# One prologue stage for the input transposes, the bias vectors, the conditioning and the first two weight blocks

## The reference

```python
proj = jnp.einsum('bsd,df->bsf', h, w_in).astype(jnp.float32)
qa, ka, va, qb, kb, vb, lr_f, lr_b, gate = _split(proj, (A_WIDTH, A_WIDTH, A_WIDTH, B_K_WIDTH, ...))
oa = dilated_attention(heads(qa, A_HEADS), heads(ka, A_HEADS), heads(va, A_HEADS), rel_bias)
...
bias = jnp.transpose(rel_bias.astype(jnp.float32)[_t5_bucket(off * dilation)], (2, 0, 1))
s = jnp.einsum('brnqhe,brnkhe->brnhqk', qs, kb) * (E ** -0.5) + bias
```

## Time and profile before

| | |
|---|---|
| median of 3 runs | 4393.03 us (4392.2 to 4393.21) |
| profiled execution | 4389.74 us, span 4388.0 us |
| TensorE, matmul busy | 3691.0 us, 84% of the span |
| VectorE / ScalarE / GpSimd busy | 1654.2 / 1069.0 / 1010.2 us |
| `tin`: first issue to last copy | 0.83 to 24.33 us |
| `bv`: first issue to the issue of the next stage | 25.04 to 35.32 us |
| `cond`: the same | 35.32 to 39.48 us |
| `in0`: first issue, first matmul | 39.48 us, 44.84 us |
| mean granted TensorE clock | 0.909 |

### The profile page before, as it was taken

One profiled execution on the slowest core, in us unless ns is written; L12 is line 12 of the kernel. 1 busy time (PEld: TensorE's weight loads), 2 busy tenths in 40 slices (PEclk: granted clock), 3 DMA queues, 4 the chain that ended last, 5 costly groups with the idle time before them and its releaser, 6 DMA issues. The chain is left out here.

```text
span 4388.0 us, 47384 instructions
## 1 busy us (share of the span) xinstructions
PE 3691.0 (84%) x16689; PEld 2400.1 (55%) x16689; DVE 1654.2 (38%) x3948; ACT 1069.0 (24%) x2172; POOL 1010.2 (23%) x844
## 2 busy tenths in 40 slices
PE   7989997887889999999998798976877835667996
PEld 3645776666445666756667346463557735333442
DVE  1025552332441343354451450063479447131101
ACT  0023433331332233233331440022214101111111
POOL 0000001332331333343342451001312534111110
PEclk8999998999999999999999897997988858888998
DMA  3164532223421111111112522253325520445996
GB/s 107 58 177 137 166 99 87 89 68 110 170 106 55 48 51 47 46 48 35 47 56 90 203 108 81 75 156 94 110 79 164 180 85 25 168 182 182 319 324 222
DMA packets 423889, 510.55 MB, mean 116 GB/s; under 512 B 71778, under 2 KB 327290, under 8 KB 423667
## 3 DMA queue, kind: packets, MB, share of 16 engines
q1 hardware_dynamic: 390067, 467.26, 32.3%
q10 hardware_dynamic: 28992, 23.65, 1.6%
q0 software_dynamic: 4608, 16.78, 1.5%
HBM read 372.94 MB, written 134.66 MB: 116 GB/s over the span
## 5 line engine op out<-in xcount | busy, mean ns | idle before, releaser
L634 PE MATMUL hgrn_ps_w<-xT,hgrn_ring 128*128 128x512 f32 x1152 | 509.8, 598 | 0.0
L606 POOL TENSOR_TENSOR hgrn_queries<-hgrn_qd,hgrn_pair_decay 128x640 f32<-128x640 f32 x192 | 285.0, 1502 | 418.2 <-PE hgrn_ps_a L685 200.0
L634 PEld LDWEIGHTS hgrn_ps_w<-xT,hgrn_ring 128*128 128x128 f32 x1152 | 218.1, 193 | 252.9 <-issue 252.8
L630 PE MATMUL hgrn_ps_w<-hgrn_ring,xT 128*128 128x256 f32 x1536 | 337.8, 379 | 0.0
L630 PEld LDWEIGHTS hgrn_ps_w<-hgrn_ring,xT 128*128 128x128 f32 x1536 | 289.2, 190 | 38.0 <-issue 0.5
L786 DVE COPY_PREDICATED hgrn_scores<-hgrn_mask,hgrn_ps_s 128x128 f32<-128x128 uint32 x192 | 48.6, 297 | 474.1 <-issue 470.3
L358 PE MATMUL gla_bg_ps<-gla_bg_w,xT 128*128 128x256 f32 x768 | 195.9, 402 | 5.2 <-DMA gla_bg_w<-in_w_in_ab_dram 5.2
L358 PEld LDWEIGHTS gla_bg_ps<-gla_bg_w,xT 128*128 128x128 f32 x768 | 151.6, 202 | 38.5 <-issue 10.6
L1151 PE MATMUL end_ps_z<-end_w,end_yT 128*128 128x512 f32 x384 | 169.2, 601 | 1.6 <-ACT end_yT L1100 1.6
L2298 PE MATMUL end_ps_z<-end_w,end_yT 128*128 128x512 f32 x384 | 168.1, 598 | 0.8 <-ACT end_yT L2226 0.8
L884 ACT ACTIVATE hgrn_k_tok<-hgrn_ps_a 128x256 f32<-128x256 f32 x84 | 32.2, 383 | 549.8 <-PE hgrn_ps_a L660 549.8
(11 more groups left out here) (597 smaller groups left out, 6865.3 us busy)
## 6 DMA issues: line engine op xcount, KB each, us to landing
expw_wg<-in_exp_w_gate_dram SPq DMA_DIRECT2D x16, 2048.0 KB, 11.1
expw_wu<-in_exp_w_up_dram SPq DMA_DIRECT2D x16, 2048.0 KB, 16.3
expw_wd<-in_exp_w_down_dram SPq DMA_DIRECT2D x16, 2048.0 KB, 21.9
att_w_ada<-in_ada_w_dram SPq DMA_DIRECT2D x24, 1024.0 KB, 5.9
hgrn_ring<-in_w_in_c_dram SPq DMA_DIRECT2D x36, 512.0 KB, 4.1
end_gt<-gate_l SPq DMA_DIRECT2D x16, 768.0 KB, 7.3
hgrn_ring<-in_w_in_c_dram SPq DMA_DIRECT2D x12, 1024.0 KB, 5.5
hgrn_o<-hgrn_o_stage SPq DMA_DIRECT2D x192, 64.0 KB, 2.7
```

Source lines behind the costliest of these rows:

```text
L606: pool.tensor_tensor(queries[:, d, s, :].rearrange("p (b a c) -> p b a c", b=POINTS, a=PC), q, f, ALU.mult).then_inc(queries_done, 1)
L630: last = pe.matmul(bank[:, q * 2 * P:(q + 1) * 2 * P], xT[:, k, t * P:(t + 1) * P], wt[:, k, :], start=(k == 0), stop=(k == KB - 1))
L634: last = pe.matmul(bank[:, :], wt[:, k, 0:P], xT[:, k, part * BANK:(part + 1) * BANK], start=(k == 0), stop=(k == KB - 1))
```

## The change

The first three stages become one, `prologue`, which also loads the two first weight blocks of the projection. All 8 tiles of `x` have a buffer of their own and are issued at once, then the two weight blocks, `c` and `c_ctx`, and, once POOL has cleared the tile, the four blocks of zero rows, all from SP's queue. The bias table and the indicators are loaded from ScalarE's queue. TensorE uses 5 banks for the transposes and 3 for the bias matmuls, which stand behind tile 4. VectorE copies the even banks and ScalarE the odd ones. POOL sets the zeros and the row of ones. ScalarE does the SiLU behind its copies, then issues the store of `vectors` and waits for all five stores; SP waits for the weights. `project` gets the loaded buffers: it skips the loads of units 0 and 1 and shifts the counts of its waits for weights.

```diff
-def transpose_in(nc, tag, src, dst, rows):
+def prologue(nc, tag, src, dst, rel_bias, buckets, vectors, vpad, c, c_ctx, sT, weights, wbuf):
...
+        @block.sync
+        def _(sp):
+            for t in range(T):
+                sp.dma_start(raw[:, t, :], src[t * P:(t + 1) * P, :]).then_inc(raw_loaded[t], 16)
+            for b in range(2):
+                sp.dma_start(wbuf[b][:, :, :], weights.rearrange("(k p) n -> p k n", p=P)[:, :, b * W:(b + 1) * W]).then_inc(w_loaded, 16)
+            with nc.allow_non_contiguous_dma(reason="a vector goes down the partitions"):
+                sp.dma_start(cond[:, 0, :], c[0].rearrange("(k p) -> p k", p=P)).then_inc(cond_loaded, 16)
+                sp.dma_start(cond[:, 1, :], c_ctx.rearrange("(k p) -> p k", p=P)).then_inc(cond_loaded, 16)
+            sp.wait_ge(zeroed, 2)
+            for first in (0, P, VPAD + SEQ, VPAD + SEQ + P):
+                sp.dma_start(vpad[first:first + P, :], zero[:, :]).then_inc(stored, 16)
+            sp.wait_ge(w_loaded, 32)
...
+            pool.memset(zero[:, :], 0.0).then_inc(zeroed, 1)
+            pool.drain()
+            pool.memset(rb[REL_BUCKETS:REL_BUCKETS + 1, :], 1.0).then_inc(zeroed, 1)
+
+        @block.scalar
+        def _(act):
+            act.dma_start(rb[0:REL_BUCKETS, :], rel_bias).then_inc(bias_loaded, 16)
+            act.dma_start(bk[:, :], buckets).then_inc(bias_loaded, 16)
             for t in range(T):
...
+                n = 2 * t + 1
+                act.wait_ge(turned, n + 1)
+                act.activation(dst[:, 4:8, t * P:(t + 1) * P], ps[n % 5][:, :].rearrange("p (j c) -> p j c", j=4), ACT.Copy).then_inc(act_copied, 1)
+            act.wait_ge(cond_loaded, 32)
+            act.activation(sT[:, :, :], cond[:, :, :].rearrange("p r k -> p k r"), ACT.Silu)
+            act.wait_ge(scaled, 3)
+            act.dma_start(vectors, vec[:, :]).then_inc(stored, 16)
+            act.wait_ge(stored, 80)
...
+                if t == MIDDLE:
+                    pe.wait_ge(bias_loaded, 32)
+                    pe.wait_ge(zeroed, 2)
+                    for n in range(3):
+                        pe.matmul(ps_v[n][0:AH, 0:VEC], rb[:, :], bk[:, n * VEC:(n + 1) * VEC], start=True, stop=True).then_inc(made, 1)
...
-def project(nc, tag, jobs, columns=None):
+def project(nc, tag, jobs, columns=None, loaded=None):
...
-        wbuf = [sb(f"wbuf{b}", [P, KB, W]) for b in range(2)]
+        wbuf = loaded or [sb(f"wbuf{b}", [P, KB, W]) for b in range(2)]
+        held = 2 if loaded else 0
...
+                if u < held:
+                    return
...
-                wait(pe, w_loaded[u % 2], 16 * i + 16 * (u // 2 + 1))
+                wait(pe, w_loaded[u % 2], 16 * i + 16 * (u // 2 + 1) - 8 * held)
```

More of the change, by code:

```diff
@@ L49, in make_identity @@
     pool.drain()
-def transpose_in(nc, tag, src, dst, rows):
-    T = rows // P
+def prologue(nc, tag, src, dst, rel_bias, buckets, vectors, vpad, c, c_ctx, sT, weights, wbuf):
+    T = SEQ // P
+    W = wbuf[0].shape[2]
     with ExitStack() as ctx:
@@ L57, in transpose_in @@
         sem = own_semaphores(nc, ctx, tag)
[L58 removed]
+        raw = sb("raw", [P, T, D])
         ident = sb("ident", [P, P])
[L60 to L63 removed]
+        rb, bk = sb("rb", [REL_BUCKETS + 1, AH]), sb("bk", [REL_BUCKETS + 1, 3 * VEC])
+        zero = sb("zero", [P, AH * AE])
+        vec = sb("vec", [AH, 3 * VEC])
+        cond = sb("cond", [P, 2, KB])
+        ps = [ctx.enter_context(nc.psum_tensor(f"{tag}_ps{b}", [P, BANK], F32)) for b in range(5)]
+        ps_v = [ctx.enter_context(nc.psum_tensor(f"{tag}_ps_v{n}", [P, BANK], F32)) for n in range(3)]
+        raw_loaded = [sem(f"raw_loaded{t}") for t in range(T)]
+        ident_ready, turned, dve_copied, act_copied = sem("ident_ready"), sem("turned"), sem("dve_copied"), sem("act_copied")
+        bias_loaded, zeroed, made, scaled, stored = sem("bias_loaded"), sem("zeroed"), sem("made"), sem("scaled"), sem("stored")
+        cond_loaded, w_loaded = sem("cond_loaded"), sem("w_loaded")
+        block = ctx.enter_context(nc.Block())
+        MIDDLE = T // 2
+        @block.sync
[11 more added lines that the diff above has]
+            sp.wait_ge(w_loaded, 32)
         @block.gpsimd
@@ L92, in _ @@
             for t in range(T):
[L93 to L97, removed]
+                n = 2 * t
+                dve.wait_ge(turned, n + 1)
+                dve.tensor_copy(dst[:, 0:4, t * P:(t + 1) * P], ps[n % 5][:, :].rearrange("p (j c) -> p j c", j=4)).then_inc(dve_copied, 1)
+                if t == MIDDLE + 1:
+                    for n in range(3):
+                        dve.wait_ge(made, n + 1)
+                        dve.tensor_scalar(vec[:, n * VEC:(n + 1) * VEC], ps_v[n][0:AH, 0:VEC], 8.0, None, ALU.mult).then_inc(scaled, 1)
 CHANNEL, TOKEN = "channel", "token"
@@ L1284, in bucket_constant @@
     return out[:, :, ::-1]
[L1287 to L1325, removed]
 def dilated_attention(nc, tag, qT, kT, vpad, vectors, attn, jobs, sT, ada_w, ada):
@@ L2056, in _ @@
             bg.move(act, LEAD + 3 * STEPS)
-def condition(nc, tag, c, c_ctx, sT):
-    with ExitStack() as ctx:
-        raw = ctx.enter_context(nc.sbuf_tensor(f"{tag}_raw", [P, 2, KB], F32))
-        loaded = own_semaphores(nc, ctx, tag)("loaded")
-        block = ctx.enter_context(nc.Block())
-        @block.sync
-        def _(sp):
-            with nc.allow_non_contiguous_dma(reason="a vector goes down the partitions"):
-                sp.dma_start(raw[:, 0, :], c[0].rearrange("(k p) -> p k", p=P)).then_inc(loaded, 16)
-                sp.dma_start(raw[:, 1, :], c_ctx.rearrange("(k p) -> p k", p=P)).then_inc(loaded, 16)
-        @block.scalar
-        def _(act):
-            act.wait_ge(loaded, 32)
-            act.activation(sT[:, :, :], raw[:, :, :].rearrange("p r k -> p k r"), ACT.Silu)
 def close_and_modulate(nc, tag, x, x_next, hT, context, hcT, o, gate, gain, w_out, ln_gain, ln_bias, alpha, norm_g, ada, ada_bias):
@@ L4421, in network @@
         gla_o = [dram(f"gla_o{d}", SEQ, B) for d in range(2)]
-        bias_vectors(nc, "bv", rel_bias, buckets, vectors, vpad)
         with nc.sbuf_tensor("sT", [P, KB, 2], F32) as sT:
-            condition(nc, "cond", c_2, c_ctx_2, sT)
             w = w_in_ab[0]
-            project(nc, "in0", [
-                Job(CHANNEL, xT, SEQ, w, 0, 256, 2, qa),
-                Job(CHANNEL, xT, SEQ, w, A, 256, 2, ka),
-                Job(TOKEN, xT, SEQ, w, 2 * A, 256, 2, vpad[VPAD:VPAD + SEQ, :]),
-            ])
+            with ExitStack() as first_weights:
+                wbuf = [first_weights.enter_context(nc.sbuf_tensor(f"in0_wbuf{b}", [P, KB, 256], F32)) for b in range(2)]
+                prologue(nc, "pro", x[0], xT, rel_bias, buckets, vectors, vpad, c_2, c_ctx_2, sT, w, wbuf)
+                project(nc, "in0", [
+                    Job(CHANNEL, xT, SEQ, w, 0, 256, 2, qa),
+                    Job(CHANNEL, xT, SEQ, w, A, 256, 2, ka),
+                    Job(TOKEN, xT, SEQ, w, 2 * A, 256, 2, vpad[VPAD:VPAD + SEQ, :]),
+                ], loaded=wbuf)
             dilated_attention(nc, "att", qa, ka, vpad, vectors, attn, [
```

14 lines of the change are left out of this document (5 added, 9 removed).

## The result

The changed kernel takes 4372.3 us in the median of 5 runs (4368.24 to 4374.15), the kernel before 4393.21 us beside it (4392.2 to 4406.97). The ratio is 0.9944, with a 95% interval of 0.9929 to 0.996: faster by more than 0.2%, as forecast. The forecast was 4373.2 us with a range of 4369.5 to 4380. The median lies 0.9 us from it. The ratio applied to 4393.03 gives 4368.4 us, 1.1 us under the range's lower end; its interval reaches from 4361.8 to 4375.5 us. So the size of the gain by that ratio, 24.6 us, exceeds the 19.8 us of the forecast, and the question for the runs was whether the part of the kernel that changed gives more than was worked out, or whether something behind it moves.

A forecast was written before the change was run, and what follows sets the result against it. Prologue waits were taken to delay the first projection matmul to 44.84 us; one full queue's transfers, a 0.5 us hole and 0.8 for the barrier gave about 25 us, 19.8 earlier: 4393.03 - 19.8 = 4373.2 us, range 4369.5 to 4380.

The forecast's parts named there:

- What bounds the prologue: Before the first projection matmul at 44.84 us: SP waits 15.7 us for two tile buffers, then small DMA latencies, weights 5.36 us.
- The sum: New prologue: bytes of SP's queue added in order of issue, to 24.1 us, plus 0.8 for the barrier; first matmul 25 us.
- the hole of 0.5: SP's queue in the prologue: zero rows issued late while SP is held by the full queue; bounded by 0 and 1.2 us.
- Other work beside the queue: Prologue: TensorE done at about 16 us or, at the lower clock, 23.2 with its last copy; copies, memset and SiLU hidden.
- the bound of 3.4: Prologue copies: splitting them between VectorE and ScalarE is worth up to 3.4 us without the cover of the later transfers.
- The slow start: First projection matmuls: lower clock level again, about 0.86 us each instead of 0.43, for some 3.6 us, as before.
- warm start: Projection's start: if TensorE came at the higher clock level, up to 1.8 us more gain.
- Slow transfers: Rival, prologue queue: deep queues move only 289 GB/s, first matmul at 32.4 us, gain 12.4 us, 4380.6 us; chance 0.15.
- everything at the best rate: Rival, prologue queue: all bytes at 427 GB/s without a hole, first matmul at 22.5 us, 4369 us with warm start; chance 0.06.
- the elements that don't fit in: Rival, prologue queue: the 2048 single elements cost 12 us instead of 1.1, about 4387 us; chance 0.05.
- the slower clock: Rival, projection: lower clock stays, each matmul 0.43 us more; 4401 us if low for a third of it; chance 0.04.
- The figure of 358 GB/s: Prologue's loads of x: the skill's HBM limit would make x take 11.7 us instead of 10.3, total 4374.6 us.

## Why the prediction was right or wrong, point by point

**What bounds the prologue.** Right. SP's wait for buffers was worth 7.9 us by itself, and the end of the new prologue is the end of SP's queue, shown by taking things out of it: 1.7 us for the elements, 3.1 us for the zero rows, and by the weight blocks, whose transfer is paid wherever they are loaded.

**The sum.** Right in its result, 25 us forecast and 25.42 measured. x was in at about 13.5 us (13.6 with the indicators). The weights took 6.0 us at their rate (5.9). Taking the elements out moved the start by 1.7 (1.1 and the hole of 0.5), the zero rows by 3.1 (3.0). The queue was over at 24.0 to 24.1 us, as the sum said. One term on the path was too small: from the end of the queue to the first matmul 1.3 to 1.4 us passed, where 0.8 stood. The 0.8 was taken from a stage that ended with an engine, and was short there too: from ScalarE's last instruction to the first matmul 1.05 us pass in the kernel with the zero rows later (21.28 to 22.33). The rest is the time until a store is known to have landed, which was left out, though the earlier trace rows had shown 1.6 us of waiting for the one of `vectors`. Off the path was tile 0: used at 5.43 us instead of 4.22, and at 4.35 to 5.43 in the merged kernels. The seven tiles queued behind it don't explain it, as with eight buffers alone it was used at 4.29; what does is not shown, and it was hidden.

**Other work beside the queue.** Right: TensorE ended at 16.87 us between the forecast ends of 16 and 22.3, the split of the copies is worth nothing in this kernel, and without the cover 1.3 us, within the bound of 3.4. That bound took two copies of 0.86 us for a tile; with TensorE at its faster pace VectorE needed 1.29 us for both, no more than the pace of arrival. ScalarE loads its table twice in the changed kernel, ahead of its first copy and ahead of the SiLU (17.52 us), 1.28 us each, both beside transfers. The store of `vectors` moved from 22.9 to 23.8 us, beside the last zero rows and not behind them; as it was issued at 21.35 us, while the issue of their last block still ran (until 21.55), this does not tell whether the two queues took turns.

**The slow start.** Right that it stays, a little short: the lower level lasted from 25.42 to about 30.2 us against 44.84 to 48.4, and the shift fell from 19.4 to 18.8 us by the attention stage. In one later execution it lasted 2.8 us only and the shift grew instead, to 20.2. The term of up to 1.8 us for a warm start had the right size: 1.7 us in the one trace that shows it.

**Slow transfers, everything at the best rate, the elements that don't fit in, the slower clock.** None came. The figure of 358 GB/s did not bind either. By the Trainium skill, DMA: Bandwidth & Descriptors, table of figures at the top, about 358 GB/s is the HBM limit of a core; its section Bandwidth says that this is what each core gets when both cores of an HBM domain stream. The trace does not show such a limit for x, 4 MB in rows of 4 KB at 403 GB/s over ten windows, with one core running. The weights, in rows of 1 KB, ran at 349, but nothing here tells whether HBM or the rows set that.

**The range: where it was wrong.** The step that failed is the lower end. It was built from cases of the first matmul alone (22.5 us with a warm start, which gave 4369, to 28 us, and slow transfers beyond). Its mechanism did not fail: the first matmul moved by 19.4 us, forecast 19.8. What the range put at nothing, without a reason, is the scatter of executions behind the prologue, and as far as the runs tell it is this that carries the measured 4368.4 us below 4369.5. The first three runs of before lay within 1.0 us. All 66 runs of it lay between 4379.71 and 4406.97 us; two traces of it differ by 8.3 us in the span, 7.9 of them between two stages more than 3200 us behind the change; and the kernel against itself came out at 0.9992. The further comparisons of the changed kernel, 0.9949 and 0.9955, stand for 4370.6 and 4373.3 us, both inside the range: that the first fell outside is chance as much as the 0.9 us between the medians is luck. An estimate from the three ratios, which lie 4.8 us apart: a range on the ratio of so few runs needs some 5 us on both sides for scatter alone, and the lower end had been 4364.5 us. A lasting gain of 1 to 3 us behind the prologue stays open.

Not foreseen was the better version: the prediction priced each transfer in the queue, and did not ask which of them the first unit needs. Only the first weight block is, and the version that waits for no more of the queue than that starts 6.7 us earlier, with ratios of 0.9928 and 0.9934.

## What to carry to other kernels

When stages are merged so that one DMA queue stays full, the new stage lasts as long as its bytes: add them up at the rates of the trace, in the order of issue, and take out of the barrier's reach whatever the next stage's first instruction does not need. Loading ahead gains nothing when the loaded bytes stand in the sum that ends the stage. Before giving a range to a few tenths of a per cent, look for how far two executions of the same program lie apart behind the change, and not only at the spread of three runs.

## What the runs showed of the hardware that was not expected

One VectorE subtraction of two tiles of 128 by 384 (L3821) took 6.6 to 7.4 us in three traces of fifteen, where the median is 0.56, and in the trace shown it ended 0.4 us behind a row of ten GpSimd products. The profile puts the matmul that waits for it down to "issue". The 66 runs of the kernel before spread over 27 us, 0.62%.

TensorE's granted clock fell after a pause of 1.94 us, stayed after one of 1.44 us, and fell 1.2 us into new work after one of 1.40 us. The lower level behind the pause of some 9 us lasted 4.8 us in one execution of the changed kernel, 5.3 in the second and 2.8 in the third.

Rows of 4 KB moved from HBM at 403 GB/s for 10 us on end, rows of 1 KB at 349; 2048 single elements cost 1.7 us in a full queue, against 3.3 us from issue to use alone. From the last packet of the zero rows to the next stage's first matmul 1.3 to 1.4 us pass in each of the five traces whose prologue ends with them.
